# Latent attention as a written-out pipeline over eight head pairs, with the rotary part of the key rotated once and the output product placed between the last attentions

## What is computed

```python
def latent_attention(x, pos, w_in, q_a_gain, w_q_up, kv_a_gain, w_kv_up, q_gain, k_gain, w_out):
    h = x @ w_in                                   # 1024 -> 384 + 256 + 32
    c_q, c_kv, k_rope = h[..., :384], h[..., 384:640], h[..., 640:]
    q = (rmsnorm(c_q, q_a_gain) @ w_q_up).reshape(B, S, 16, 96)
    kv = (rmsnorm(c_kv, kv_a_gain) @ w_kv_up).reshape(B, S, 16, 64 + 64)
    k_nope, v = kv[..., :64], kv[..., 64:]
    k = concatenate([k_nope, broadcast_to(k_rope, (B, S, 16, 32))])
    q, k = rmsnorm(q, q_gain), rmsnorm(k, k_gain)
    q = concatenate([q[..., :64], rope(q[..., 64:], pos)])
    k = concatenate([k[..., :64], rope(k[..., 64:], pos)])
    o = softmax(causal(q @ k.T * 96 ** -0.5)) @ v   # per head
    return o.reshape(B, S, 1024) @ w_out
```

## Time and profile before

| | us |
|---|---|
| median of 3 runs | 2034.5 (2033.71 to 2038.77) |
| the profiled execution | 2033.73 |
| its span in the trace | 2031.6 |
| first product of the down projection | 1637.53 |
| first projection of a head pair (line 848) | 1660.88 |
| first product of the output (line 770) | 1799.48 |
| last addition to X begins (line 779) | 1829.07 |

### The profile page before, as it was taken

The page is one execution under the profiler, slowest core; times in us unless marked ns, Lnnn a source line. Parts: engine busy times, 40 slices in busy tenths (PEclk is TensorE's granted clock), DMA queues, the critical chain, the costliest instruction groups (busy, mean ns, idle before and its releaser), DMA issues.

```text
span 2031.6 us, 30209 instructions
## 1 busy us (share of the span) xinstructions
PE 1885.8 (93%) x11572; PEld 1446.8 (71%) x11572; DVE 913.3 (45%) x1358; ACT 742.1 (37%) x1223; POOL 101.5 (5%) x99
## 2 busy tenths in 40 slices
PE   5999699999999889998999998999899967788998
PEld 2876444443443389988999977999899955548998
DVE  4242322222221364447778744445554435515554
ACT  3252122211221244445555534443444434414443
POOL 1010000000000000001212110000000011100000
PEclk8999799999999989999999999999999987879999
DMA  9864399999999956656654524664666530205663
GB/s 370 303 208 185 153 421 422 422 422 422 422 422 422 347 156 186 186 168 177 189 141 125 138 63 125 186 185 128 201 183 183 190 148 1 62 0 158 184 185 114
DMA packets 316357, 441.85 MB, mean 217 GB/s; under 512 B 10757, under 2 KB 269445, under 8 KB 288389
## 3 DMA queue, kind: packets, MB, share of 16 engines
q1 hardware_dynamic: 313464, 431.59, 61.4%
q0 software_dynamic: 2560, 8.40, 1.3%
q10 hardware_dynamic: 272, 1.05, 0.1%
HBM read 439.95 MB, written 1.05 MB: 217 GB/s over the span
## 4 chain that ended last, share of the span: by engine, by line
PE 77%; DMA 14%; DVE 4%; ACT 3%; issue 1%; POOL 1%; SPq 0%; ACTq 0%; DVEq 0%; POOLq 0%
PE PS L245 24%; DMA R<-w_up 13%; PE PS L255 12%; PE PS L442 10%; PE PS L1892 6%; PE PS L1559 4%; PE PS L1953 2%; PE PS L770 1%; PE PS L722 1%; PE PS L1668 1%; PE PS L1872 1%; PE PS L514 1%; PE PS L848 1%; PE PS L358 1%; DMA R<-w_ada 1%
## 5 line engine op out<-in xcount | busy, mean ns | idle before, releaser
L245 PE MATMUL PS<-XH,HI 128*128 128x256 f32 x1408 | 399.9, 284 | 0.6 <-DVE LO L179 0.6
L245 PE MATMUL PS<-XL,HI 128*128 128x256 f32 x1408 | 398.4, 283 | 0.0
L245 PE MATMUL PS<-XH,LO 128*128 128x256 f32 x1408 | 398.4, 283 | 0.0
L245 PEld LDWEIGHTS PS<-XH,HI 128*128 128x128 f32 x1408 | 270.2, 192 | 5.0 <-DVE LO L179 1.3
L245 PEld LDWEIGHTS PS<-XL,HI 128*128 128x128 f32 x1408 | 270.1, 192 | 3.8
L245 PEld LDWEIGHTS PS<-XH,LO 128*128 128x128 f32 x1408 | 270.1, 192 | 0.0
L179 DVE TENSOR_TENSOR LO<-RAW,HI 128x2048 fp32r<-128x2048 f32 x88 | 201.7, 2292 | 116.6 <-ACT HI L175 116.6
L188 ACT ACTIVATE HI<-RAW 128x1024 fp32r<-128x1024 f32 x88 | 93.4, 1062 | 293.9 <-PE PS L255 293.9
L212 DVE TENSOR_TENSOR LO<-RAW,HI 128x1024 fp32r<-128x1024 f32 x88 | 107.8, 1225 | 195.7 <-ACT HI L188 195.5
L1892 PE MATMUL PS<-SPLIT,ARENA 128*64 128x512 f32 x512 | 170.0, 594 | 13.1 <-DMA R<-w_up 13.1
L175 ACT ACTIVATE HI<-RAW 128x2048 fp32r<-128x2048 f32 x88 | 167.8, 1907 | 2.6 <-DMA RAW<-ffn_w_in 1.6
(11 more groups left out here) (328 smaller groups left out, 3033.2 us busy)
## 6 DMA issues: line engine op xcount, KB each, us to landing
RAW<-ffn_w_in SPq DMA_DIRECT2D x176, 512.0 KB, 5.1
R<-w_down SPq DMA_DIRECT2D x64, 1024.0 KB, 17.6
RAW<-w_gate SPq DMA_DIRECT2D x48, 1024.0 KB, 20.3
SPLIT<-w_up SPq DMA_DIRECT2D x48, 1024.0 KB, 23.5
RAW<-ffn_w_out SPq DMA_DIRECT2D x88, 512.0 KB, 3.6
RAW<-a_w_in SPq DMA_DIRECT2D x72, 512.0 KB, 5.4
R<-w_ada SPq DMA_DIRECT2D x24, 1024.0 KB, 7.6
SPLIT<-w_gate SPq DMA_DIRECT2D x16, 1024.0 KB, 23.5
```

The source lines that it names most:

```text
L245: m = e.matmul(GU[j][:, T * q:T * q + T], gu(w, j)[:, q, k, :], x[:, k, :], start=(k == 0 and n == 0), stop=(k == KT - 1 and n == 2))
```

## The change

The diff is in `latent`, in the buffers that it uses and in one line of the rotary tables. The class `Attention` goes; its steps are now functions inside `latent`, and the loops are written out for eight pairs `m`.

- The down projection is cut at 384 columns (all of the query latent) and 288; its first block starts on each `XL` slice as it comes. Squares are read out of PSUM, each position tile `t` has its own inverse roots, and VectorE scales straight from PSUM into `C` (line 942). The copy of `C` goes. Transposes go tile by tile, and the first projection waits for each slice of `CT` singly.
- The query's and key's gains of the 64 unrotated columns are multiplied into one table. The key's rotary part is multiplied and rotated once (`key_tables`, 754 to 759) into `PRE`, whose columns for it stay through all pairs; its squares likewise in `SQ`. Rotation now comes before the norm, which multiplies all of `PRE` at the end (`scale`).
- Per pair VectorE reads queries from PSUM. ScalarE makes all squares. Both projections have one bank each (0 for queries, 1 for keys and values), for both tiles. Transposes go to banks 4 and 7.
- Weights of one head (three blocks) are transposed into one bank, copied in one piece, and multiplied with the heads alternating. Values are kept for four pairs.
- The output product is cut into seven pieces among the last pairs on TensorE.

The core of the diff:

```diff
@@ pe(), the pairs @@
-        def body(i, j, further=True, following=True):
-            ni, nj = after(i, j)
-            if further:
-                project(i + 1, j)
-            if following:
-                turn(ni, nj, last=not further)
-            at.weighted(i, j, 0, 0)
-            at.weighted(i, j, 0, 1)
-            if following:
-                scores(ni, nj, 0, turned(ni, nj, not further) + 2)
-            at.weighted(i, j, 1, 0)
-            at.weighted(i, j, 1, 1)
-            if following:
-                scores(ni, nj, 1, None)
+        for n in range(PAIRS - 2):
+            if n:
+                turn_weights(n - 1)
+            scores(n)
+            project_q(n + 2)
+            project_kv(n + 2)
+            turn(n + 1)
+            if n:
+                weighted(n - 1)
+        e.wait_ge(s.wo_in, 16 * KT)
+        turn_weights(LAST - 2)
+        scores(LAST - 1)
        ...
+        out(0, range(0, 3))
+        turn(LAST)
+        out(0, range(3, 5))
+        weighted(LAST - 2)
+        turn_weights(LAST - 1)
+        scores(LAST)
        ...
+        out(1, range(0, 5))
+        weighted(LAST - 1)
        ...
+        out(2, range(0, 6))
+        out(0, range(5, 6))
+        out(1, range(5, 6))
+        turn_weights(LAST)
        ...
+        out(3, range(0, 6))
+        weighted(LAST)
+        for n in range(4):
+            out(n, range(6, 7))
+        for n in range(4):
+            out(n, range(7, 8)).then_inc(s.y_done, 1)
@@ act(), the pairs @@
+        for n in range(PAIRS + 1):
+            if n:
+                weights_out(n - 1)
+            if n < PAIRS:
+                exponent(n)
+            if n + 2 < PAIRS:
+                query_squares(n + 2)
+                keys_out(n + 2)
+            if n + 1 < PAIRS:
+                turn_out(n + 1)
+            if n:
+                output(n - 1)
@@ dve(), the pairs @@
+        for n in range(PAIRS):
+            if n + 1 < PAIRS:
+                scale(n + 1)
+            shifted(n)
+            if n + 2 < PAIRS:
+                rotate(n + 2)
+            divided(n, 0)
+            if n + 2 < PAIRS:
+                square_sums(n + 2)
+            divided(n, 1)
@@ the waits that tie the pairs together @@
+    def rotate(m):
+        n = Chain(v, s.nr, added(m) - 4)
+        v.wait_ge(s.squares, 4 * m + 1)
+    def scale(m):
+        v.wait_ge(s.rs, 2 + 2 * m + 2)
+        v.wait_ge(s.squares, 4 * m + 3)
        ...
+    def shifted(m):
+        for h in range(2):
+            if m:
+                v.wait_ge(t_.pt_full, FILLS + 2 * (m - 1) + h + 1)
+            for t in range(NT):
+                v.wait_ge(t_.sc_full, softmax_of(m, h, 1) + 1)
@@ pe(), down projection @@
+                for q, (lo, hi) in enumerate(COLS):
                     for kk in range(KH):
                         k = KH * c + kk
+                        if (c, t, q) == (0, 0, 0):
+                            e.wait_ge(M.xl_done, KT * n_norm + k + 1)
```

More of the change, by code:

```diff
@@ L943, in low, with project_q @@
                         ALU.subtract).then_inc(s.w_lo[c], 1)
+    def project_q(m):
+        if m == 0:
+            e.wait_ge(s.wq_in, 32)
+        else:
+            e.wait_ge(s.nr, added(m - 1))
+            e.wait_ge(s.squares, 4 * m - 3)
+        for t in range(NT):
+            for k in range(3):
+                if m == 0 and t == 0:
+                    e.wait_ge(s.ct_done, k + 1)
+                x = e.matmul(PS[:, 0, 2 * B_QK * t:2 * B_QK * t + 2 * B_QK], CT[:, k, 128 * t:128 * t + 128],
+                             WQ[:, k, 2 * B_QK * m:2 * B_QK * m + 2 * B_QK], start=k == 0, stop=k == 2)
+        x.then_inc(s.fb_full, 1)
@@ new lines, in project_kv, with query_squares @@
+    def project_kv(m):
+        if m == 0:
+            e.wait_ge(s.ct_done, 5)
+        else:
+            e.wait_ge(s.squares, 4 * m)
+        for t in range(NT):
+            for k in range(2):
+                x = e.matmul(PS[:, 1, 256 * t:256 * t + 256], CT[:, 3 + k, 128 * t:128 * t + 128],
+                             WKV[:, k, 256 * m:256 * m + 256], start=k == 0, stop=k == 1)
+        x.then_inc(s.fb_full, 1)
+    def query_squares(m):
+        a.wait_ge(s.fb_full, 2 * m + 1)
+        at_least(a, s.nr, summed(m - 1) if m else 0)
+        a.activation(SQ[:, :, 0:2], QB, ACT.Square).then_inc(s.squares, 1)
@@ new lines, in turn_out, with scores @@
+    def turn_out(m):
+        for t in range(NT):
+            a.wait_ge(s.qt_full, 2 * m + t + 1)
+            if m:
+                a.wait_ge(t_.sc_full, softmax_of(m - 1, 1, 1) + 1)
+            a.activation(QKT[:, :, 128 * t:128 * t + 128], TB[t][0:B_QK, :].rearrange("p (h n) -> p h n", h=4),
+                         ACT.Copy).then_inc(s.qt_done, 1)
+    def scores(m):
+        e.wait_ge(s.qt_done, 2 * m + 2)
+        for h in range(2):
+            if m:
+                e.wait_ge(t_.sc_read, softmax_of(m - 1, h, 1) + 1)
+            for t in range(NT):
+                e.matmul(SCORES[h][t], QKT[:, h, 128 * t:128 * t + 128], QKT[:, 2 + h, 0:128 * t + 128],
+                         start=True, stop=True).then_inc(t_.sc_full, 1)
@@ new lines, in out @@
+        def out(n, ks):
+            t, q = divmod(n, 2)
+            for k in ks:
+                e.wait_ge(t_.o_free, OUTS + k + 1)
+                x = e.matmul(YB[n], M.OT[:, k, 128 * t:128 * t + 128], wo_at(k)[:, 512 * q:512 * q + 512],
+                             start=k == 0, stop=k == KT - 1)
+            return x
+        for m in range(2):
+            project_q(m)
+            project_kv(m)
+        turn(0)
+        for n in range(PAIRS - 2):
[7 more added lines that the diff above has]
+                weighted(n - 1)
```

520 lines of the change are left out of this document (185 added, 335 removed).

## The result

| | before | changed |
|---|---|---|
| median, us (lowest to highest) | 2036.63 (2033.71 to 2039.76) | 1957.64 (1956.48 to 1961.93) |
| profiled execution, us | 2033.73 | 1957.86 |
| its span, us | 2031.6 | 1956.0 |

The ratio is 0.9616, with a 95% interval from 0.9601 to 0.963: faster by 79 us in the medians and 75.9 between the two profiled executions, where 69.6 were forecast against the profiled one.

What follows compares the result with a forecast made beforehand. Bound: PE's own line of work, idle in each pair's chain and partly at 1.2 GHz. Terms: -62.6 us from first projection to last addition, -4.1 and -2.9 ahead, giving 1964.1, 1965 for a median; range 1955 to 1986.

Steps and rivals of the forecast that it cites:

- The ring: Middle pairs: sum, root, scaling, shift, exponentials, queries' squares, rotation, division and next sum follow each other in 9.0 us.
- The granted clock in the six loops: Sign to look for in the middle pairs' profile: a granted clock of 0.95 or more.
- Squares directly behind the last exponential: Sign in the middle pairs: the query's squares directly follow the last exponential, with the rotation behind them.
- The last stretch: From the end of the last sum to the last addition: PE has no stop, 36.3 us.
- The loop: Middle pairs, from one pair's sum to the next: 9.0 us against 15.2, bounds 8.6 and 10; six loops 54 us.
- my upper bound of 10: Slow bound in us for a middle pair's loop: 0.1 us for each of ten hand-overs that the rows don't show.
- The clock by the first weights: First loop: PE idles before the first weights, then starts at the low level; 1.8 us lost, up to 3.0 or none.
- P: Start of the first pair's projection, from which later times are counted; forecast near 1654.
- The rival (a fall in every loop, 1983): Middle pairs: clock falls in each loop, loop 12.0, 18 us more; chance 0.22 for falls in some or all loops.
- Filling: From the first pair's projection to the end of the second pair's sum: 13.5 us.
- Down projection: Start of the down projection: begins on the first XL slice instead of all eight, gain 2.9 us, all kept.
- From there to P: From the down projection's end to the first pair's projection: 4.2 us instead of 8.3, gain 4.1, bounds 3 to 5.

Runs made afterwards that it cites:

- values_early: Changed kernel with each pair's weights-by-values products directly behind their transposes, ahead of the next pair's scores: 1965.68 us, ratio 0.965.
- sum_twice: Changed kernel with a second, unused sum over the 768 squared columns in each pair, directly ahead of the first: 1970.58 us, ratio 0.9673.
- one_root: Changed kernel with one root over four columns behind both tiles' squares, in place of one root per tile: 1964.02 us, ratio 0.9646.
- after_again: Changed kernel once more with nothing edited, measured and profiled a second time: 1958.40 us, ratio 0.9615.
- keys_each: Changed kernel with the keys' rotary part rotated and squared anew for every pair instead of once: 1967.25 us, ratio 0.9654.

## Why the prediction was right, and where it was not

**Right in mechanism.** The ring is the one that was written down, every step in it, in that order; adding to it, adding beside it and shortening it each did what the ring says (+0.86, 0.00 and -0.73 us a loop). Squares directly behind the last exponential and the rotation behind them were to show it, and do. The last stretch came to 36.55 for 36.3. The granted clock in the six loops is 1.00, where 0.95 or more was forecast for the middle pairs.

**The loop, 9.0 for 8.33**, is the largest miss: 4.0 us in six. Most is in two terms. The division was taken as 0.85 from the earlier trace rows, where each reciprocal is followed by its scaling; with both reciprocals first it is 0.65. From the shifts to the rotation I counted the exponentials whole and then 0.52 for squares: the squares start 0.1 us before the last accumulator is read, and take 0.47. Hand-overs that the rows don't show cost 0.05 us at most (the root, 2.20 for 2.15): my upper bound of 10 had been ten of 0.1.

**The clock by the first weights, 1.8 us** in the sum, was 0 in the profiled execution and 2.4 in the other one. The step was right to keep 0 to 3, and no single value is right. But the stop that it was put on was misread: I let TensorE stand from P+19 to P+23.4, when head 1's weights are divided. Head 0's are divided ahead of the sum, and the trace has two stops, of 1.60 and 0.97 us. That the range holds is in part luck. The rival (a fall in every loop, 1983) didn't come: behind the second loop no execution of the changed kernel's order showed a fall, with 0.64 us of idle time a loop, where I had put 1 to 1.6. In values_early, with 1.6 us of idle time in two stops, it didn't either. So a fall in every loop was given too much within its 0.22; a fall in one loop, which that chance also covers, is common. That it can fall once is shown: of the twelve profiled executions with the new loop or an edit of it seven lost nothing, five lost something once (sum_twice, one_root and after_again about 2.4 us, keys_each 2.7, values_early 4.2), and none twice.

**Filling, 13.5 for 11.5.** The step that failed is the first: "The first pair's last keys leave PSUM at 1667.68, P+6.8". In the changed kernel the keys' squares begin at P+4.9. The views of these two pieces, of the kernel before and of the changed one, say why:

```profile
1660.88:1667.68 6.80, 6.80 (x21) 6.17 (x22) 0.00 (x0) 1.25 (x5) 0.00 (x0) 0.58 0.00 0
```

```profile
1655.42:1660.34 4.92, 4.88 (x20) 4.33 (x20) 1.10 (x4) 1.80 (x5) 0.00 (x0) 0.80 0.00 0
```

TensorE had no stop before either, so the old staging in banks didn't set that time. The clock did: 6.80 us at 0.58 and 4.92 at 0.80 are both 3.9 us of work at the full level. In after_again, where the level is full from P on, the keys' squares begin at P+4.0. I took over a time without the clock at which it was made, so this gain depends on the level too, and none of it is shown to come from the new banks.

**Down projection, 2.9 for 1.6.** I let TensorE begin with the first XL slice at 1634.5. But its own transposes of the norm end at 1635.9, and the products stand behind them in its queue. They start at 1635.57, 2.2 us earlier against the XL slices than before, and the first ones are slow (the granted clock is 0.52 up to 1636.97):

```profile
1632.24 3.68 PE L136 MATMUL PS<-ID,ARENA 128*128 128x128 f32 x16 [5.93 <-DVE ARENA L123]
...
1636.04 0.52 PE L977 MATMUL PS<-LO,XH 128*128 128x384 f32 x1
...
1637.67 0.34 PE L977 MATMUL PS<-HI,XH 128*128 128x384 f32 x1
```

I had costed when VectorE has the slices ready and not the queue of the engine itself. The low part of chunk 1 ended at 1642.1 and held nothing up, as forecast.

**From there to P, 4.2 for 4.16.** The two scalings out of PSUM took 1.00 us together, for 0.97 forecast and 0.63 had they run as out of SBUF:

```profile
1653.41 1.00 DVE L942 TENSOR_SCALAR ARENA<-PS,RSB 128x384 f32<-128x384 f32 x2
```

So what the Trainium skill says (VectorE: DVE Perf Modes, Why PSUM operands drop a tier) holds here too. The change gains all the same: the copy that it saves had taken 0.79 us, the slower read costs 0.37. (The row of 425 ns for 256 columns that the forecast compared is a shift with a mask, which reads two tensors, so it was no clean measure of PSUM; the size came out right all the same.)

The sum of the misses: 5.8 (loops and clock) + 2.0 (filling) - 1.3 (down projection) - 0.2 (last stretch) = 6.3 us, the difference between 69.6 and 75.9.

**What stays open:** why a stop is followed by a fall of the clock in one execution and not in another: all that is known here is that it varies. And of 51.4 us of overlap I have priced parts (values 1.2 a loop, output 5.5, keys 0.7 a pair), not the whole: a version in which no pair overlaps wasn't made.

## What to carry to other kernels

When a pipeline's loop is the question, write down the ring of waits and test it by adding one operation in it and the same one beside it; the loop moves by the whole of the first and by nothing of the second. When an engine is to start earlier, look at what stands in its own queue, and take no time over from a row without the granted clock of its stretch. And where TensorE has to wait anyway, transposes of the identity into unread columns kept the clock up and took 19 us off the stretch of a kernel that was otherwise untouched.

## What the hardware showed that I had not expected

The cost of the clock's level isn't a property of the kernel alone: the same stops cost 0 or 2.4 us in the loop behind them, and the down projection's start ran at the low level for between 0 and 5.6 us. And two VectorE operations without a wait between them overlap: both reciprocals take 0.21 us where single ones take 0.16, and with the two grouped a head's division takes 0.65 us, where the forecast from rows of the old order had 0.85.
